# A two-layer float32 block on one core: residual stream turned to tokens on partitions, norms by ScalarE sums and PE transposes

## The reference, cut to what matters

```
def rms_norm(x, g):                       # over the 2048 features of a token
    return x * lax.rsqrt(jnp.mean(x * x, axis=-1, keepdims=True) + 1e-6) * g

x = x + cat(conformer(rms_norm(x, even_norm) @ even_w_in), attention(...)) @ even_w_out     # even_w_in 2048x7168
x = x + (sparse_attention(rms_norm(x, odd_norm) @ odd_w_in) * silu(gate)) @ odd_w_out       # latent attention
x = rms_norm(x, final_norm)                                                                 # the block's last norm
h = rms_norm(x, g_mix_2)                                                                    # and at once the next
x = x + (gate_a * delta_net(h @ w_in_2) + gate_f * fourier(h @ w_in_2)) @ w_o_2
h = rms_norm(x, g_mlp_2)
x = x + jnp.square(jax.nn.relu(h @ w_mlp_up_2)) @ w_mlp_down_2                              # 2048 -> 8192 -> 2048
return rms_norm(x, g_final_2)
```

## Time and profile before

| | us |
|---|---|
| median of 3 runs | 2507.71 (2498.87, 2507.71, 2511.86) |
| profiled execution | 2511.18, of which the span is 2509.2 |
| busy: PE, POOL, DVE, ACT | 2352.9, 1725.9, 1242.9, 1033.4 |
| 716 units at POOL (L500) | 1725.5, 2.419 each |
| moved by DMA | 378.16 MB read, 2.10 MB written, mean 152 GB/s |

### The profile page before, as it was taken

The page is one execution under the profiler, slowest core; times in us unless marked ns, Lnnn a source line. Parts: engine busy times, 40 slices in busy tenths (PEclk is TensorE's granted clock), DMA queues, the critical chain, the costliest instruction groups (busy, mean ns, idle before and its releaser), DMA issues.

```text
span 2509.2 us, 37814 instructions
## 1 busy us (share of the span) xinstructions
PE 2352.9 (94%) x13235; PEld 2027.5 (81%) x13235; DVE 1242.9 (50%) x1884; ACT 1033.4 (41%) x1332; POOL 1725.9 (69%) x723
## 2 busy tenths in 40 slices
PE   6999996989889797999999999998999999999997
PEld 5888884877677685788888888887888888888886
DVE  3156647332654336136657473533663753643644
ACT  3344453334345434343535354443333333333332
POOL 3888872658455573655657574886898888888883
...
GB/s 146 193 185 188 186 161 58 134 134 147 116 110 118 108 207 72 138 128 133 143 111 159 110 159 93 196 188 151 151 193 191 187 189 186 185 185 185 189 186 84
DMA packets 382784, 381.67 MB, mean 152 GB/s; under 512 B 14551, under 2 KB 379998, under 8 KB 382430
## 3 DMA queue, kind: packets, MB, share of 16 engines
...
HBM read 378.16 MB, written 2.10 MB: 152 GB/s over the span
## 4 chain that ended last, share of the span: by engine, by line
PE 84%; DVE 8%; ACT 3%; issue 2%; POOL 1%; ACTq 1%; DVEq 0%; POOLq 0%
PE lin_ps L1668 48%; PE lin_ps L1670 24%; PE ps L1639 2%; POOL w_lo L500 1%; DVE scr L933 1%; ACT w_hi L533 1%; PE ps L2033 1%; DVE a L945 1%; ACT a L574 1%; PE ps L2026 1%; PE ps L1952 1%; PE ps L2032 1%; PE ps L1889 1%; DVE stat L1238 0%; DVE z L1235 0%
## 5 line engine op out<-in xcount | busy, mean ns | idle before, releaser
L500 POOL TENSOR_TENSOR w_lo<-raw,w_hi 128x1024 fp32r<-128x1024 f32 x716 | 1725.5, 2419 | 745.4 <-ACT w_hi L533 421.8
L1668 PE MATMUL lin_ps<-a,w_hi 128*128 128x512 f32 x3584 | 1290.1, 403 | 41.4 <-DVE a L945 24.0
L1670 PE MATMUL lin_ps<-a,w_lo 128*128 128x256 f32 x3584 | 1009.4, 282 | 0.0
L1668 PEld LDWEIGHTS lin_ps<-a,w_hi 128*128 128x128 f32 x3584 | 679.4, 190 | 212.2 <-issue 30.3
L1668 PE MATMUL lin_ps<-b,w_hi 128*128 128x512 f32 x1952 | 691.4, 399 | 8.5 <-issue 4.4
L1670 PEld LDWEIGHTS lin_ps<-a,w_lo 128*128 128x128 f32 x3584 | 683.6, 191 | 2.7 <-issue 1.9
L544 ACT ACTIVATE w_hi<-raw 128x1024 fp32r<-128x1024 f32 x388 | 410.5, 1061 | 661.8 <-PE lin_ps L1670 642.6
L1670 PE MATMUL lin_ps<-b,w_lo 128*128 128x256 f32 x1952 | 548.7, 281 | 0.0
L1668 PEld LDWEIGHTS lin_ps<-b,w_hi 128*128 128x128 f32 x1952 | 368.8, 189 | 99.1 <-issue 5.1
L1670 PEld LDWEIGHTS lin_ps<-b,w_lo 128*128 128x128 f32 x1952 | 371.0, 190 | 0.1
L533 ACT ACTIVATE w_hi<-raw 128x1024 fp32r<-128x1024 f32 x232 | 240.8, 1055 | 262.8 <-PE lin_ps L1670 243.4
...
## 6 DMA issues: line engine op xcount, KB each, us to landing
...
raw<-in_w_mlp_up SPq DMA_DIRECT2D x128, 512.0 KB, 3.7
raw<-in_w_mlp_down SPq DMA_DIRECT2D x128, 512.0 KB, 3.3
...
```

The source lines that it names most:

```text
L500: nc.gpsimd.tensor_tensor(w_lo[:, slot], raw[:, slot], w_hi[:, slot].bitcast(F32), ALU.subtract).then_inc(lo_done, 1)
L1668: nc.tensor.matmul(acc, hi[:, k, m * P:(m + 1) * P], src[:, kk].rearrange("p s n -> p (s n)"), start=(q == 0 and k == 0), stop=False)
L1670: last = nc.tensor.matmul(acc[:, 0:T], lo[:, k, m * P:(m + 1) * P], src[:, kk, 0, :], start=False, stop=(q == n - 1 and k == UK - 1))
```

## The change

The residual becomes token-major, `[128 partitions, 2, 2048]` (half q of the tokens, then features), and with it:
- **Projections.** The seven matrix products that add to `x` (`even_w_out`, `odd_w_out`, `w_o_2` and the four quarters of `w_mlp_down_2`) go through the new `projected`: activations still, 512 columns of weights moving. A unit is now 2 chunks x 512 outputs, 12 matmuls of 512 columns; four blocks of 8 units replace eight groups of 4. `to_x` adds a PSUM block to `x` in one instruction per q. All code of `projected` is written out, without a loop.
- **Norms.** ACT squares each block of `x` as it is finished, with the sum over features as `accum_out`; root and reciprocal have one value per token. The scaling is one DVE (q=0) and one ACT (q=1) instruction per block; 32 PE transposes (`turn_block`) bring it feature-major into `ps`, 16 of them ahead of the first matmul; ACT writes the rounded part with the gain (`upper`), DVE the remainder (`lower`), 256 columns each. `preload` loads ACT's root table ahead.
- **Two norms in one.** For `final_norm` and `g_mix_2`, DVE adds the block in PSUM, ACT squares it, DVE multiplies by the gain into `x`, ACT squares again (`to_x_gains`); one scaling serves both, and the first norm's factor reaches `x` later, in `w_o_2`'s `to_x`. `mlp3` and `g_final_2` go the same way, then the scaled `x` is written out directly, 8 DMAs of 256 KB, with no transpose.
- **Order.** At the start `x` is loaded by 8 DMAs of ACT's queue into place; the constants move from ACT's queue to SP's, behind the first unit. The DMAs of tables behind `odd_w_out` move from SP's queue to ACT's, inside the projection. The first four units of `odd_w_out` are copied ahead of the last round's silu, and the first three of the next layer inside each projection. Projection weights load in rows of 2 KB instead of 1 KB.

```diff
-         (64, 66, 66, 66), (66, 68, 68, 68))
+         (64, 66, 66, 66), (66, 68, 68, 70))
...
-        x = sb("x", [P, DC, T])
+        x = sb("x", [P, TT, D])
...
+            def stream_out(name, u0, row0=0):
+
+                v = t[name].rearrange("(k p) n -> p k n", p=P)
+                with sp.Fori(0, NB) as i:
+                    col = sp.snap(i * BLK)
+                    for j in range(8):
+                        slot = (u0 + j) % SLOTS
+                        sp.wait_ge(lo_done, i * 8 + (u0 + j - SLOTS + 1))
+                        sp.dma_start(raw[:, slot].rearrange("p (k n) -> p k n", k=2),
+                                     v[:, row0 + 2 * j:row0 + 2 * j + 2, bass.ds(col, BLK)]).then_inc(raw_in[slot], 16)
...
-            sp.dma_start(lmask, t["c_lmask"].bitcast(BF16)[:, 0:5]).then_inc(table_in, 16)
-            sp.dma_start(dmask[:], t["c_dmask"].bitcast(BF16)).then_inc(table_in, 16)
...
+            stream_out("odd_w_out", UNIT0["odd_w_out"])
...
+            for n in range(NB):
+                for q in range(TT):
+                    sp.wait_ge(fin_done[q], n + 1)
+                    sp.dma_start(out[q * P:(q + 1) * P, _block(n)], x[:, q, _block(n)]).then_inc(out_done, 16)
...
+            for n in range(NB):
+                for q in range(TT):
+                    act.dma_start(x[:, q, _block(n)], t["x"][q * P:(q + 1) * P, _block(n)]).then_inc(x_in[n], 16)
...
+            def squares(r, n):
+
+                for q in range(TT):
+                    if n:
+                        act.wait_ge(nm_sq.sem, nm_sq.at(f"s{n - 1}{q}", r))
+                    nc.scalar.activation(scr[:, q, :], x[:, q, _block(n)], ACT.Square,
+                                         accum_out=sq_sum[:, 2 * n + q:2 * n + q + 1]).then_inc(nm_sq.sem, 1)
...
+            def roots_of(r):
+                act.wait_ge(nm_rs.sem, nm_rs.at("rest", r))
+                for q in range(TT):
+                    act.wait_ge(nm_sq.sem, nm_sq.at(f"s{NB - 1}{q}", r))
+                    nc.scalar.activation(root[:, q:q + 1], sq_sum[:, 2 * (NB - 1) + q:2 * (NB - 1) + q + 1], ACT.Sqrt,
+                                         bias=rest[:, q:q + 1], scale=1.0 / D).then_inc(nm_sq.sem, 1)
...
+            def norm(r, u0, first=False):
+
+                def scale(n):
+                    if n >= 2:
+                        act.wait_ge(nm_pe.sem, nm_pe.at(f"{2 * n - 3}", r))
+                    nc.scalar.activation(scr[:, 2 * (n % 2) + 1, :], x[:, 1, _block(n)], ACT.Copy,
+                                         scale=recip[:, 1:2]).then_inc(nm_sc[1].sem, 1)
+
+                def upper(n, js=range(4)):
...
+                        act.wait_ge(nm_pe.sem, nm_pe.at(f"{c // 2}", r))
+                        g = ROWS[NORMS[r]] + c
+                        nc.scalar.activation(a[:, c, 0, :], ps[:, 2 * (n % 2) + j // 2, (j % 2) * T:(j % 2 + 1) * T], ACT.Copy,
+                                             scale=vec[:, g:g + 1]).then_inc(nm_hi.sem, 1)
...
+            def projection(name, r, n):
+
+                u0 = OUTS[name][0]
+                preload(n)
+                for j in range(4, 35):
+                    hi(u0 + j, (u0 + j) % SLOTS)
+                    if j in (12, 20, 28):
+                        added(name, (j - 12) // 8)
+                        squares(r, (j - 12) // 8)
+                added(name, NB - 1)
+                squares(r, NB - 1)
+                roots_of(r)
...
-                done_to = max(first + 1, min(end + 1, 67))
+                done_to = max(first + 1, min(end + 1, 71))
...
+            for j in range(4, 35):
+                hi(u0 + j, (u0 + j) % SLOTS)
+                if j in (12, 20, 28):
+                    added_squares(0, 2, OUTS["odd_w_out"][1], (j - 12) // 8)
+                if j in (15, 23, 31):
+                    squares2((j - 15) // 8)
+                if j == 11:
+                    for w in range(2):
...
+                    act.dma_start(gains, t["final_norm"].rearrange("(a n) -> a n", a=1).broadcast_to([P, D])).then_inc(gain_in, 16)
+                    act.dma_start(lmask, t["c_lmask"].bitcast(BF16)[:, 0:5]).then_inc(table_in, 16)
...
+            act.wait_ge(group_free, GROUP0["mix"] + 16)
+            act.dma_start(gains, t["g_final_2"].rearrange("(a n) -> a n", a=1).broadcast_to([P, D])).then_inc(gain_in, 16)
+            projection("w_o_2", 3, 3)
...
+                nc.vector.tensor_reduce(nst[:, 24:26], sq_sum.rearrange("p (n q) -> p q n", q=TT)[:, :, 0:NB - 1], AX.X,
+                                        ALU.add).then_inc(nm_red.sem, 1)
+                dve.wait_ge(nm_red.sem, nm_red.at("red", r))
+                nc.vector.tensor_scalar(rest, nst[:, 24:26], 1.0 / D, EPS, ALU.mult, ALU.add).then_inc(nm_rs.sem, 1)
...
+            def norm(r, between=None):
+
+                def scale(n):
+                    if n >= 2:
+                        dve.wait_ge(nm_pe.sem, nm_pe.at(f"{2 * n - 3}", r))
+                    nc.vector.tensor_scalar(scr[:, 2 * (n % 2), :], x[:, 0, _block(n)], recip[:, 0:1], None, ALU.mult).then_inc(nm_sc[0].sem, 1)
...
+                        dve.wait_ge(nm_hi.sem, nm_hi.at(f"{c | 1}", r))
+                        g = ROWS[NORMS[r]] + c
+                        nc.vector.scalar_tensor_tensor(out=a[:, c, 1, :], in0=ps[:, 2 * (n % 2) + j // 2, (j % 2) * T:(j % 2 + 1) * T],
+                                                       scalar=vec[:, g:g + 1], in1=a[:, c, 0, :].bitcast(F32),
+                                                       op0=ALU.mult, op1=ALU.subtract).then_inc(nm_lo.sem, 1)
+
+                reciprocals(r, 0)
+                dve.wait_ge(nm_rs.sem, nm_rs.at("rn0", r))
+                scale(0)
+                reciprocals(r, 1)
+                scale(1)
+                lower(0)
+                scale(2)
+                lower(1)
+                scale(3)
+                if between:
+                    between()
+                lower(2)
+                lower(3)
...
+            def to_x(name, r=None, scale=None):
+
+                u0, g0 = OUTS[name]
+                for n in range(NB):
+                    if r is not None and n == NB - 1:
+                        rest_of(r)
+                    dve.wait_ge(unit_used, u0 + 8 * n + 8)
+                    for q in range(TT):
+                        xs = x[:, q, _block(n)]
+                        nc.vector.scalar_tensor_tensor(out=xs, in0=xs, scalar=scale[:, q:q + 1] if scale is not None else 1.0,
+                                                       in1=lin_ps[:, 2 * ((g0 + n) % 2) + q, :], op0=ALU.mult,
+                                                       op1=ALU.add).then_inc(group_free if q else x_half, 1)
...
+                    for q in range(TT):
+                        acc = lin_ps[:, 2 * ((g0 + n) % 2) + q, :]
+                        nc.vector.tensor_tensor(acc, acc, x[:, q, _block(n)], ALU.add).then_inc(mg_dve.sem, 1)
+                    dve.wait_ge(gain_in, 16 * (rnd + 1))
+                    for q in range(TT):
+                        dve.wait_ge(nm_sq.sem, nm_sq.at(f"s{n}{q}", r))
+                        nc.vector.tensor_tensor(x[:, q, _block(n)], lin_ps[:, 2 * ((g0 + n) % 2) + q, :], gains[:, _block(n)],
+                                                ALU.mult).then_inc(group_free if q else mg_dve.sem, 1)
...
+                reciprocals(4, q)
+            dve.wait_ge(nm_rs.sem, nm_rs.at("rn0", 4))
+            for n in range(NB):
+                dve.wait_ge(mg_dve.sem, mg_dve.at(f"y0{n}", 1))
+                nc.vector.tensor_scalar(x[:, 0, _block(n)], x[:, 0, _block(n)], recip[:, 0:1], None, ALU.mult).then_inc(fin_done[0], 1)
...
+            def turn_block(r, n):
+
+                for q in range(TT):
+                    pe.wait_ge(nm_sc[q].sem, nm_sc[q].at(f"{n}", r))
+                for half in range(2):
+                    if n >= 2:
+                        pe.wait_ge(nm_lo.sem, nm_lo.at(f"{4 * (n - 2) + 2 * half + 1}", r))
+                    for j in (2 * half, 2 * half + 1):
+                        for q in range(TT):
+                            m = nc.tensor.transpose(ps[:, 2 * (n % 2) + half, (j % 2) * T + q * P:(j % 2) * T + (q + 1) * P],
+                                                    scr[:, 2 * (n % 2) + q, j * P:(j + 1) * P], ident[:])
+                    m.then_inc(nm_pe.sem, 1)
...
             def normed(r):
                 def wait(c):
-                    if c % 2 == 0:
-                        pe.wait_ge(nr_lo.sem, nr_lo.at(f"{c // 2}", SPLIT_ROUND[r]))
...
+                    if c in (4, 8):
+                        turn_block(r, c // 4 + 1)
+                    pe.wait_ge(nm_lo.sem, nm_lo.at(f"{c}", r))
+                for n in range(2):
+                    turn_block(r, n)
                 return wait
 
...
+            def projected(name, src, waits=None):
+
+                u0, g0 = OUTS[name]
+                for n in range(NB):
+                    pe.wait_ge(group_free, g0 + n - 1)
```

(16 more changed lines are left out.)

423 lines of the change are left out of this document (228 added, 195 removed).

## The result

The changed kernel takes 2402.57 us (median of 4 runs, 2396.35 to 2404.43) against 2507.09 (4 runs, 2498.87 to 2511.86): a ratio of 0.9582, 95% interval 0.9551 to 0.9613, so 104.5 us less. The forecast was 2418, with a range from 2396 to 2445.

A forecast was written before the change was run, and what follows sets the result against it. PE bounds the kernel, by its pace and the holes between stretches; seven terms sum to 95.3 us, less 6 gives 89: 2511.2 to 2422 profiled, 2418 median; own range 2403 to 2431, 8 in 10 2396 to 2445.

The forecast's parts named there:

- 6 us set against: Deduction from the summed gains: transposes do not raise PE's clock, so four seams may each keep about 1.5 us more half clock.
- Start: Kernel's start: first matmul at 18 against 34.37, first group done at 33 to 35 against 51.36; 17 us (14 to 20).
- `even_w_out`'s seam: Norm's hole before the odd layer: shorter, but `cq` stalls some 2 us at its fifth unit; 10.5 us (7 to 12).
- `odd_w_out`'s start: Weight copies ahead of the last silu remove PE's 4.44 us idle and half clock behind it; 6 us (4 to 7).
- Double norm: Two norms after `odd_w_out` become one: 19.6 us at the first matmul, some 7 us wait at group 3; net 18 (12 to 24).
- `w_o_2`'s seam: Norm behind `w_o_2`: first matmul 8.7 us after T0 against 16.9, PE no longer starved; 12.4 us (9 to 13).
- End: From T0 of the last block to the span's end: about 12 us against 29.6; gain 17.6 (13.5 to 20).
- Form: Projections: 896 fewer matmuls with the same columns, at 13 to 17 ns each; 13.8 us, bounds 0 and 19.
- the second: Rival: seams give back about 20 us as DVE's scalings wait for POOL and half clock lasts longer; 2438, chance 0.10.
- The first and third: Rivals in the projections: first, the form gives nothing, 2433, chance 0.10; third, slower matmuls, 2552, chance 0.04.
- The fourth: Rival: start and end bound by DMA, `x` landing at 16, output draining in 10 us; 10 less, 2428, chance 0.06.

The follow-up runs named there:

- split experiment: Changed kernel with the middle of the projections' three products issued as two matmuls of 256 columns, 16 per unit: 2413.16 us, ratio to before 0.9616.

## Why the prediction was right, and where its sizes were off

The mechanism is the one forecast, and most of the seven terms came out larger. They add up to 107.9 us in the two profiles, where 95.3 were forecast, and the 6 us set against them did not come. The rest of the 114.7 is the second group at the start and the pace of `even_w_in`. The median, 2402.57, is 15.4 below the forecast: inside the range for 8 in 10, and just below the forecast's own range (2403 to 2431). The kernel before has one profile, so a term is sure to 1 or 2 us at best; what the changed kernel's other two profiles give is said where it differs.

- *Start*, 17: 17.1 at the first group; the first matmul came at 19.66 and not at 18, the group within 33 to 35 as said. Two things are not in the sum: a copy of a weight unit on ACT ahead of the last block's squares (1.0 us), and DVE's first scaling waiting for POOL (0.6 us). The second group gave 1.6 more.
- *`even_w_out`'s seam*, 10.5: 13.6, from T0 to a matmul of the odd attention that waits for DVE in both (540.52 to 640.64, and 512.93 to 599.41); 12.7 and 12.3 with the other two profiles. The stall in `cq` was 1.96 us, as said, though ahead of its sixth unit and not its fifth (behind 60 matmuls). The term had set the gain too low from T0 on: the first matmul came at +7.6, not +8.7, and at nearly full clock (at +7.2 and +7.3 and at half clock in the other two).
- *`odd_w_out`'s start*, 6: 5.3 (7.0 less the form's 1.7; 6.9 and 5.3 with the other two), and 6.0 to 7.5 by the experiment that undid it.
- *Double norm*, 18: 20.8 (19.9 and 20.8 with the other two). The first matmul came at T0 + 8.8 and not 10.5. PE then waited 5.6 us at the third group, where the step had 7, and moving the masks took the wait away. But one premise was wrong: the masks do not begin when the norm ends. DVE first waited 5.1 us for ACT's late copy, and L1488 with the masks then took 13.6 us and not 15; the wait came out near the forecast by luck.
- *`w_o_2`'s seam*, 12.4: 13.5 (14.1 and 13.4 with the other two). The chain was the one laid out, and each link somewhat shorter: the squares 0.61 us apart and not 0.8, the roots 0.23 and not 0.3, the scalings 0.48 and not 0.7, the transposes 0.21 and not 0.23. The experiments put 2.4 us on the early squares and 1.4 on the early table.
- *End*, 17.6: 18.8. The eight issues took 4.49 us, not 6.9.
- *Form*, 13.8: 18.8 is what the distances give (4 projections of 22.62 and 3 of 22.18 us per block, all now 21.76: 4 x 3.4 + 3 x 1.7). That is the upper bound that the prediction gave, and for its reason. The 13.8 was mis-sized by taking one price per matmul removed; the projections also left the slower of the two paces of the 512-and-256 form, which three MLP quarters and `even_w_out` had had in this profile. The split experiment gives the price per matmul alone, 16.7 ns, so 15 us.
- *The 6 us set against the sum*: this step failed. It said that transposes do not bring the clock up and would cost 1.5 us more in each seam. The transposes did run at half clock (3.65 us for 16). But by the granted clock of the three inner seams, full clock came between 0.3 us ahead of the first weight matmul and 1.3 us behind it (up to 1.8 in the two repeated profiles, up to 2.7 in the experiments'), where it had come 2.8 to 5.4 us behind it before. The 6 us also counted twice what the term for `w_o_2` already held: transposes at half clock's pace and 2 us of half clock behind them. At the double norm the first matmul already runs at full clock in two of the three profiles (its row answers to 973.07 of the earlier trace rows, 0.77 long):
```profile
899.34 3.52 PE L1830 MATMUL ps<-ident,scr 128*128 128x128 f32 x16 [5.54 <-ACT scr L614]
902.61 0.47 PE L1859 MATMUL lin_ps<-a,w_hi 128*128 128x512 f32 x1
```
  The trace of before showed it too. The window of the earlier trace rows that the step rests on, 2500 to 2503, stops too early: the same run of 24 transposes, with nothing else on PE, goes on at half clock and ends at full.
```profile
2503.00:2505.00 2.00, 1.98 (x11) 1.47 (x10) 1.38 (x2) 0.00 (x0) 0.00 (x0) 0.50 0.81 268
2505.10:2506.00 0.90, 0.52 (x5) 0.28 (x3) 0.78 (x2) 0.00 (x0) 0.00 (x0) 1.00 0.93 305
```
  What the Trainium skill says in "TensorE: Matmul & The Clock Gate", section "Part 4: PE-mode transpose", that this mode does not count as busy for the clock in the same way, is not borne out here.
- Of the rivals, the second (which the prediction once calls the third) did not come in the inner seams, by the order: its lock exists (scalings of 1.13 and 1.18 us when POOL was made busy), but in the kernel POOL has nothing to do at that point, with three units copied ahead and the fourth not yet. That bears out the Trainium skill, "SBUF — State Buffer", section "Who interferes with whom", which counts `tensor_scalar` among the operations that can take the shared ports with a single SBUF operand. The prediction said that this case agrees for two operands only; but the trace of before had one with a single operand, L1306, a TENSOR_SCALAR among the masks, 2.42 us. The first and third are out: 226.7 ns per matmul. The fourth is out too: `x` had landed by 12.6 us, when ACT squares its last block, and the end takes 10.8 us in all.
- The profiled spans differ by 114.7 us and the medians by 104.5, as the profile of before had the slow pace in `even_w_in` and that of the changed kernel the quick one. With the slow pace in both, as in the repeated profile (2401.4), it is 107.8. The profiled execution of before is also 4 us above its median, and that of the changed kernel 6 below.
